# Experts of a mixture layer ranked by token count on the chip, with full jobs of 128 slots and half jobs of 64 slots in turn

## The reference

```python
def _swiglu(h, w_gate, w_up, w_down):
    return (jax.nn.silu(h @ w_gate) * (h @ w_up)) @ w_down

def _moe(h, w_router, b_router, w_gate, w_up, w_down):
    logits = (h @ w_router).astype(jnp.float32) + b_router.astype(jnp.float32)
    top_vals, top_idx = lax.top_k(logits, TOP_K)
    wts = jax.nn.softmax(top_vals, axis=-1)
    combine = jnp.sum(jax.nn.one_hot(top_idx, N_EXPERTS) * wts[..., None], axis=-2)
    out = jnp.zeros_like(h)
    for e in range(N_EXPERTS):
        out = out + combine[..., e:e + 1] * _swiglu(h, w_gate[e], w_up[e], w_down[e])
    return out
```

## Time and profile before

| | value |
|---|---|
| runs | 2107.23, 2112.40, 2112.99 us; median 2112.4 |
| the profiled execution: span from first to last instruction | 2107.7 us |
| TensorE busy (matmul) | 2035.7 us, 97% |
| VectorE busy | 1439.6 us, 68% |
| ScalarE busy | 1148.5 us, 54% |
| GpSimd busy | 130.5 us, 6% |
| moved by DMA | 526.67 MB, mean 250 GB/s |
| granted TensorE clock, mean | 0.992 |
| a job, from one output to the next | 97.9 to 98.0 us |

### The profile page before, as it was taken

One profiled execution on the slowest core, in us unless ns is written; L12 is line 12 of the kernel. 1 busy time (PEld: TensorE's weight loads), 2 busy tenths in 40 slices (PEclk: granted clock), 3 DMA queues, 4 the chain that ended last, 5 costly groups with the idle time before them and its releaser, 6 DMA issues. The chain is left out here.

```text
span 2107.7 us, 34719 instructions
## 1 busy us (share of the span) xinstructions
PE 2035.7 (97%) x13413; PEld 1830.5 (87%) x13413; DVE 1439.6 (68%) x1595; ACT 1148.5 (54%) x1162; POOL 130.5 (6%) x170
## 2 busy tenths in 40 slices
PE   7999999999999999999999899999999999999997
PEld 5999999888999889989999688888888888888885
DVE  4477445555444455755454699898989898988987
ACT  4433334444333443432443568686868677776865
POOL 3100003200000030000230100000000000000000
PEclk9999999999999999999999999999999999999998
DMA  9634465654766454435654599999999999999996
GB/s 352 213 91 155 129 205 174 203 179 131 219 200 215 136 164 147 122 103 171 184 184 164 189 325 398 327 393 328 380 347 367 358 349 376 326 394 319 403 326 252
DMA packets 244081, 526.67 MB, mean 250 GB/s; under 512 B 18151, under 2 KB 142169, under 8 KB 243970
## 3 DMA queue, kind: packets, MB, share of 16 engines
q1 hardware_dynamic: 234304, 495.78, 67.0%
q0 software_dynamic: 9648, 29.29, 4.5%
q10 hardware_dynamic: 18, 0.04, 0.0%
HBM read 512.44 MB, written 12.59 MB: 249 GB/s over the span
## 5 line engine op out<-in xcount | busy, mean ns | idle before, releaser
L1688 ACT ACTIVATE mhi<-mraw 128x2048 fp32r<-128x2048 f32 (+1 forms) x318 | 574.0, 1819 | 210.5 <-DMA mraw<-in_w_exp_up 72.9
L1157 DVE TENSOR_TENSOR mlo<-mraw,mhi 128x2048 fp32r<-128x2048 f32 (+1 forms) x317 | 677.1, 2163 | 15.7 <-ACT mhi L1688 14.8
L571 DVE TENSOR_TENSOR wlo<-raw,whi 128x1024 fp32r<-128x1024 f32 x244 | 289.1, 1212 | 314.8 <-ACT whi L1397 313.6
L1973 PE MATMUL ps<-h1h,whi 128*128 128x320 f32 x1248 | 385.1, 321 | 8.8 <-DVE h1l L678 3.9
L1974 PE MATMUL ps<-h1l,whi 128*128 128x320 f32 x1248 | 370.7, 309 | 0.0
L2469 PE MATMUL ps<-mhi,xeh 128*128 128x512 f32 (+1 forms) x864 | 326.7, 378 | 1.8 <-DVE xel L1176 1.7
L2470 PE MATMUL ps<-mhi,xel 128*128 128x512 f32 (+1 forms) x864 | 321.3, 372 | 0.0
L1397 ACT ACTIVATE whi<-raw 128x1024 fp32r<-128x1024 f32 x244 | 247.8, 1046 | 118.9 <-PE ps L2358 44.9
L1973 PEld LDWEIGHTS ps<-h1h,whi 128*128 128x128 f32 x1248 | 235.3, 189 | 25.3 <-issue 18.7
L1974 PEld LDWEIGHTS ps<-h1l,whi 128*128 128x128 f32 x1248 | 235.5, 189 | 0.0
L2475 PE MATMUL ps<-mlo,xeh 128*128 128x512 f32 (+1 forms) x864 | 224.5, 371 | 0.0
(11 more groups left out here) (415 smaller groups left out, 2657.1 us busy)
## 6 DMA issues: line engine op xcount, KB each, us to landing
mraw<-in_w_exp_down SPq DMA_DIRECT2D x198, 512.0 KB, 8.6
mraw<-in_w_exp_gate SPq DMA_DIRECT2D x150, 512.0 KB, 5.5
mraw<-in_w_exp_up SPq DMA_DIRECT2D x144, 512.0 KB, 6.5
raw<-in_w_in SPq DMA_DIRECT2D x128, 512.0 KB, 3.9
raw<-in_w_ada SPq DMA_DIRECT2D x64, 512.0 KB, 3.8
mraw<-in_w_exp_gate SPq DMA_DIRECT2D x72, 384.0 KB, 3.6
mraw<-in_w_exp_up SPq DMA_DIRECT2D x72, 384.0 KB, 4.6
pause<-in_w_ada SPq DMA_DIRECT2D x32, 512.0 KB, 6.8
```

Of the source, the lines that this page charges most:

```text
L571: V.tensor_tensor(WLO[:, u % RAW_UNITS, 0:w], RAW[:, u % RAW_UNITS, 0:w], WHI[:, h % HI_UNITS, 0:w].bitcast(F32), ALU.subtract).then_inc(l ...
L1157: V.tensor_tensor(MLO[:, n % RAW_RING, 0:w], MRAW[:, n % RAW_RING, 0:w], MHI[:, n % HI_RING, 0:w].bitcast(F32), ALU.subtract).then_inc(m_l ...
L1688: A.activation(MHI[:, n % HI_RING, 0:w], MRAW[:, n % RAW_RING, 0:w], ACT.Copy).then_inc(m_hi, 1)
L1973: M.matmul(out_, w, v[0], start=start, stop=False, skip_group_check=True)
```

## The change

1. The seven experts 1 to 7 are ranked by count on the chip. Job 0 is expert 0 as before, with 128 slots. Jobs 2, 4, 6 take the three fullest with 128 slots; jobs 1, 3, 5, 7 the four others with 64 slots (`half`). An expert with more tokens than its slots gets extra jobs of 64 slots (`EXTRA` = 6). Job 7 is run by the conditional loop, which has 1 + `EXTRA` turns.
2. In a half job the high part of the 64 gathered rows stands in columns 0 to 63 of the stationary operand and the low part in columns 64 to 127. One pass over the weights' high part so gives both; with the pass over the low part there are 2 passes in place of 3. Rows 0 to 63 and 64 to 127 of the result are still to be added: the "turn" product multiplies by `FOLD` (two stacked identities) in place of the identity, which adds them while it transposes. So in a half job gate and up are copied raw from PSUM by ScalarE (`SG`, `SU`), folded by TensorE, and silu, the product with up and the split are done on the folded tiles of 64 columns. `choose` for a half job compares with slot numbers 0 to 63, twice over (`IOTAH`).
3. The table of jobs takes nine parts and not five, and starts at pair 2; SyncE waits for it before job 1 and reads the expert of every job.

The diff, cut to what the prediction speaks of:

```diff
-EXTRA = 4
+HALF = 64
+MAIN = NE - 1
+EXTRA = 6
 JOBS = NE + EXTRA
+TURNS = 6
...
-TABLE_PAIRS = {17: 0, 20: 1, 22: 2, 25: 3, 28: 4}
+TABLE_PAIRS = {2: 0, 4: 1, 6: 2, 8: 3, 17: 4, 19: 5, 21: 6, 23: 7, 25: 8}
...
             sp.wait_ge(sem("routed"), 1)
-            extra = sp.value_load(XI[0:1, 4:5], min_val=0, max_val=EXTRA)
-            with sp.Fori(0, EXTRA) as k:
+            with sp.Fori(0, MAIN // 2) as two:
+                for job in (two * 2 + 1, two * 2 + 2):
+                    e = sp.value_load(XI[0:1, bass.ds(job, 1)], min_val=0, max_val=NE - 1)
+                    load_job(job, e)
...
-            def choose(job):
-
+            def choose(job, half):
+
+                slots = IOTAH[:, :] if half else CF[:, C_IOTA:C_IOTA + P]
                 for t in range(TT):
-                    V.tensor_scalar(PM[:, t, :], CF[:, C_IOTA:C_IOTA + P], POSJ[:, t, bass.ds(job, 1)], None,
-                                    ALU.is_equal)
+                    V.tensor_scalar(PM[:, t, :], slots, POSJ[:, t, bass.ds(job, 1)], None, ALU.is_equal)
...
+                if half:
+                    V.tensor_tensor(XEH[:, s, HALF:P], src[:, :, HALF:P], XEH[:, s, 0:HALF].bitcast(F32),
+                                    ALU.subtract).then_inc(xe_out, 1)
...
+            def half_constants():
+
+
+                V.tensor_tensor(FOLD[:, :], CF[:, C_ID:C_ID + HALF], CF[:, C_ID + HALF:C_ID + P], ALU.add)\
+                    .then_inc(sem("fold_made"), 1)
+                V.tensor_copy(IOTAH[:, 0:HALF], CF[:, C_IOTA:C_IOTA + HALF])
+                V.tensor_copy(IOTAH[:, HALF:P], CF[:, C_IOTA:C_IOTA + HALF])
                 V.memset(PRE[:, :, :], 0.0)
-                V.tensor_scalar(CNT[:, 1, :], CNT[:, 0, :], float(P), None, ALU.is_gt)
-                st(V.tensor_scalar(CNT[:, 2, :], CNT[:, 0, :], float(2 * P), None, ALU.is_gt))
-                V.tensor_tensor(CNT[:, 3, :], CNT[:, 1, :], CNT[:, 2, :], ALU.add)
-                st(V.tensor_tensor(PRE[:, 0, 9:16], CNT[:, 1, 0:7], CNT[:, 2, 0:7], ALU.add))
+                V.memset(XF[:, :], 0.0)
+                st(V.scalar_tensor_tensor(KEY[:, 0, :], CNT[:, 0, :], float(NE), CF[:, C_IOTA8:C_IOTA8 + NE],
+                                          ALU.mult, ALU.subtract))
...
+                n = [P, NE, NE]
+                st(V.tensor_tensor(OH[:, 0], KEY[:, 0:1, :].broadcast_to(n), KEY[:, 0, :].unsqueeze(2).broadcast_to(n),
+                                   ALU.is_gt))
+                st(V.tensor_reduce(KEY[:, 1, :], OH[:, 0], AX.X, ALU.add))
+                st(V.tensor_scalar(KEY[:, 2, :], KEY[:, 1, :], 3.5, None, ALU.is_gt))
+                st(V.tensor_scalar(KEY[:, 3, :], KEY[:, 2, :], 7.0, None, ALU.mult))
+                st(V.scalar_tensor_tensor(KEY[:, 3, :], KEY[:, 1, :], 2.0, KEY[:, 3, :], ALU.mult, ALU.subtract))
...
+            def half_low(job, number, k):
+
+
+                f0, nf = tile_at(k)
+                dve.wait_ge(gt_hi, job * TURNS + (k + 1))
+                V.tensor_tensor(GTH[:, f0:f0 + nf, HALF:P],
+                                SGT[:, k % 2, 0:nf * HALF].rearrange("p (k n) -> p k n", k=nf),
+                                GTH[:, f0:f0 + nf, 0:HALF].bitcast(F32), ALU.subtract).then_inc(half_lo, 1)
...
+                        elif what == "turn" and half:
+                            n = tile_at(k)[1] * HALF
+                            dve.wait_ge(gate_out, job * TURNS + (k + 1))
+                            V.tensor_tensor(SGT[:, k % 2, 0:n], SGT[:, k % 2, 0:n], PS[:, bank, 256:256 + n], ALU.mult)\
                                 .then_inc(m_aux_out, 1)
...
-            with dve.Fori(1, NE) as job:
-                job_dve(job)
+            job_dve(0, False, True, first=True)
+            with dve.Fori(0, MAIN // 2) as two:
+                job_dve(two * 2 + 1, True, False, two)
+                job_dve(two * 2 + 2, False, True)
             dve.wait_ge(sem("routed"), 1)
-            extra = dve.value_load(XI[0:1, 4:5], min_val=0, max_val=EXTRA)
-            with dve.Fori(0, EXTRA) as k:
+            extra = dve.value_load(XI[0:1, 15:16], min_val=1, max_val=1 + EXTRA)
+            with dve.Fori(0, 1 + EXTRA) as k:
                 with dve.If(k < extra):
-                    job_dve(k + NE)
-            dve.wait_ge(m_aux_out, extra * JAUX + (NE * JAUX + AHEAD))
-            dve.wait_ge(xe_out, extra * 2 + (NE * 2 + 2))
+                    job_dve(k + MAIN, True, True, k + MAIN // 2)
...
+            def half_high(job, k, s):
+
+
+                f0, nf = tile_at(k)
+                act.wait_ge(m_aux_out, job * JAUX + (AHEAD + s + 1))
+                A.activation(GTH[:, f0:f0 + nf, 0:HALF],
+                             SGT[:, k % 2, 0:nf * HALF].rearrange("p (k n) -> p k n", k=nf), ACT.Copy).then_inc(gt_hi, 1)
...
+                    if half and p < GPAIRS and p % KD == KD - 1:
+                        g, w = p // KD, GROUPS[p // KD][1]
+                        for i in range(2):
+                            act.wait_ge(m_tile, job * 9 + (3 * g + 1 + 2 * i))
+                            A.activation(SG[:, i, 0:w], PS[:, GROUP_BANKS[g][2 * i], 0:w], ACT.Copy)
+                            if i == 0:
+                                act.wait_ge(m_tile, job * 9 + (3 * g + 2))
+                            else:
+                                act.wait_ge(m_used, job * PAIRS + (p + 1))
+                            A.activation(SU[:, i, 0:w], PS[:, GROUP_BANKS[g][2 * i + 1], 0:w], ACT.Copy)\
+                                .then_inc(prod_made, 1)
...
+                        if what == "turn" and half:
+                            n = tile_at(k)[1] * HALF
+                            act.wait_ge(m_aux_in, job * JAUX + (s + 1))
+                            if k >= 2:
+                                act.wait_ge(half_lo, number * TURNS + (k - 1))
+                            A.activation(SGT[:, k % 2, 0:n], PS[:, 4 + s % 2, 0:n], ACT.Silu).then_inc(gate_out, 1)
...
                             M.matmul(o_, XEH[:, k, :], hi_[:, s], start=(k == 0), stop=False)
-                            M.matmul(o_, XEL[:, k, :], hi_[:, s], start=False, stop=False)
+                            if not half:
+                                M.matmul(o_, XEL[:, k, :], hi_[:, s], start=False, stop=False)
...
                                 M.matmul(PS[:, DOWN_BANKS[h], :], GTH[:, kf, :], hi_[:, s], start=(kf == 0), stop=False)
-                                M.matmul(PS[:, DOWN_BANKS[h], :], GTL[:, kf, :], hi_[:, s], start=False, stop=False)
+                                if not half:
+                                    M.matmul(PS[:, DOWN_BANKS[h], :], GTL[:, kf, :], hi_[:, s], start=False, stop=False)
...
+                            for m in range(tile_at(k)[1] if half else 0):
+                                for j, raw in enumerate((SG, SU)):
+                                    c0 = 256 * j + m * HALF
+                                    ins = M.matmul(PS[:, bank, c0:c0 + HALF], raw[:, k % 2, m * P:(m + 1) * P],
+                                                   FOLD[:, :], start=True, stop=True, skip_group_check=True)
...
```

192 lines of the change are left out of this document (123 added, 69 removed).

## The result

The changed kernel takes 2099.1 us in the median of four runs (2098.3 to 2101.7), the kernel before 2111.8 us beside it: ratio 0.9945, 95% interval 0.993 to 0.9959. It is 12.7 us faster where 36.7 were forecast, and 2099.1 lies inside the range.

A forecast was written before the change was run, and what follows sets the result against it. The prediction took TensorE to set the pace, with VectorE and DMA close behind. Five half jobs saving 48.5 us, less 1.0 for job 0 and 10.8 at the end, gave -36.7 us: 2076 us, range 2044 to 2108.

The forecast's parts named there:

- The half job's time: Step for each 64-slot job: VectorE's 83.9 us plus waits of 1.4 and 3.0 give 88.3 us, bounds 84 and 96.
- TensorE in a half job: Step on TensorE's work in a 64-slot job: it falls from 98.0 to 70.7 us and stops being the bound.
- VectorE in a half job: Step on VectorE's work in a 64-slot job: 87.4 less 8.9 plus 5.4, so 83.9 us, highest by busy time.
- The handoffs: Term in the 64-slot job: 0.5 us of waiting for each of six turned tiles passed between engines, 3.0 us.
- The data rate: Step on weight loads: 410 GB/s from the trace, 85.6 us for 35.1 MB, against the page's 358 GB/s.
- The full jobs: Step on the 128-slot jobs: nothing changes, TensorE still needs 98.0 us, no gain counted.
- The end: Term after the last job: two more leftover gathers, 9.4 us, and two more empty turns, 1.4, together 10.8 us.
- The handoffs' case: Rival for 64-slot jobs: handoffs between three nearly full engines cost twice as much, 94 us a job, 2104 in all; 17%.
- The ring's slack across jobs: Rival: the load ring carries slack between jobs, a full and a half job together take 174 us, 2026 in all; 7%.
- 348 GB/s: Rival: gate and up loads are held to this rate, 95.7 us a half job, 2113 in all, no change; 6%.
- Another count: Rival: an expert of 63 or 62 tokens exceeds 64 on the chip, a tenth job of 88 us, 2159; 2%.
- The clock: Rival: TensorE's clock falls in half jobs as it idles between pairs, 141 us a job at 1.2 GHz, 2340; 6%.

The follow-up runs named there:

- e13: Changed kernel, but in half jobs VectorE makes 32 low-part columns per block and TensorE's second pass rereads the high part: 2101.63 us, half jobs 94.1.
- e5: Changed kernel, but in half jobs each pair's second transfer brings only 128 columns, about half the bytes: 2059.49 us, half jobs 84.7.
- e14: Changed kernel, but in half jobs SyncE waits for one more used pair, a ring of six slots: 2138.42 us, half jobs 101.1.
- e11: Changed kernel, but in half jobs VectorE makes its eight adds two steps earlier: 2102.95 us, half jobs 94.9.
- e17: As e13, with ScalarE's raw copies at group ends cut to 64 columns: 2087.7 us, half jobs 90.2.
- e8: Changed kernel run again unaltered for a second profile: 2101.92 us, half jobs 93.2.
- e3b: Changed kernel with every job run as a full job of 128 slots in 3 passes: 2127.67 us, ratio 1.007 to the kernel before.
- e10: Changed kernel with the loop of three turns over two jobs written out on the four engines: 2096.88 us, ratio 0.9923 to the kernel before.
- e9: Changed kernel, but half jobs make and use the low part for 32 columns per block only, skipping the rest of the low pass: 2108.87 us, half jobs 96.5.
- e7: Changed kernel, but in half jobs TensorE runs 24 extra products into an unused bank after pair 4: 2106.29 us, half jobs 94.6.

## Why the prediction was wrong

**The step that failed is "The half job's time"**: that VectorE, highest by busy time, sets it, and that only its own handoff waits, 4.4 us, come on top. The half job is 93.4 us, 5.1 over the forecast. Five such jobs are 25.5 us, more than the 23 by which the median missed. What holds in its place: the half job is the time that 35.1 MB take through a ring of seven slots whose holder TensorE is. Shown of this are that VectorE's amount of work doesn't set it (24.5 us in place of 84.1, and the job is no shorter: e13), that the bytes count (e5), that one slot less costs 7.7 us (e14), and that the missing 7.5 us lie in the gate and up rows, where the loads run at 266 to 381 GB/s. There TensorE is late for two reasons. It stops at the adds and at the copies, and with the first stop gone the second holds the ring (e11). And between them, in pairs 10 to 19, its own work fills the time (e17). How the 7.5 us divide between the two in the changed kernel is argued, not shown. The 85.6 us of the transfers were in the prediction, but only as a time that 83.9 and its waits would cover; the error was to let the two lie over each other for a whole job. While VectorE and TensorE lag in the gate and up rows, the transfers lose time that the down rows, already at 410 GB/s, can't give back.

An estimate shows how little the ring leaves. While outputs are added, TensorE comes to pair 7 only after an add that stands behind the low part of pair 8. In e13 ScalarE begins to round pair 7 as it lands, and SyncE loads into its slot 7.8 us later; pair 15, loaded after a stop with nothing queued ahead of it, lands 5.1 us after its first issue (1912.11, shown above):

```profile
1895.41 1.92 ACT L1775 ACTIVATE mhi<-mraw 128x2048 fp32r<-128x2048 f32 x1 [0.65 <-DMA mraw<-in_w_exp_up]
...
1903.19 0.33 SPq L536 DMA_DIRECT2D mraw<-in_w_exp_gate  x1
...
1917.24 1.91 ACT L1775 ACTIVATE mhi<-mraw 128x2048 fp32r<-128x2048 f32 x1 [1.52 <-DMA mraw<-in_w_exp_up]
```

With VectorE's full low part, 2.0 us longer, a slot is thus in use for 5.1 + 7.8 + 2.0 = 14.9 us at least. At 410 GB/s seven 1.049 MB slots come round in 7 x 2.56 = 17.9 us, six in 15.4. Seven leave 3.0 us and six 0.5, and a stop of 3.7 us is more than either. That is argued, not shown.

**TensorE in a half job** was undersized. A turn of four tiles is eight products, and takes 1.70 us (in e13 from 1919.40 to 1921.10), so 22 tiles take 9.4 us and not 6.0. The trace has two instructions for each of these full-precision products, 88 for 44. So the row that the forecast divided, 4.4 us in 32, stands for 16 products:

```profile
L2652 PE MATMUL ps<-fold,su 128*128 128x64 f32 x44 | 8.5, 275 | 0.0
L2652 PE MATMUL ps<-fold,sg 128*128 128x64 f32 x44 | 8.4, 272 | 0.0
```

That makes 74 us of work and not 70.7. Sixteen of the 22 tiles are turned beside pairs 10 to 19, 6.8 us of work in the stretch where the loads run slow and TensorE is busy 5.00 of 5 us in five of the six windows. The forecast expected gaps before the low pass; a sum over the whole job hid that in this stretch there are hardly any.

**VectorE in a half job**, 83.9: right, 84.1. The turned tiles of 256 columns take 0.42 us (forecast 0.41). **ScalarE**, 77: 73.4; its busy time is no matter, its order at the copies is. **The handoffs**, 3.0: VectorE waited 2.6 + 1.8 us at turned tiles, and 3.1 us at low parts for rounded pairs, which the sum had not; the first kind is 1.1 us when less data have to come (e5).

**The data rate.** 410 was right as the rate with free slots (409 to 415 in every window from 1936 to 1971 us), and wrong as the mean. By the 358 GB/s that the Trainium skill, DMA: Bandwidth & Descriptors, Specifications, gives a core as its share, a half job would be 98.1 us, an estimate; the trace disagrees with it, with 377 in the mean and 410 where nothing holds it. Only one core runs here, and no run shows two.

**The full jobs**, nothing: 97.0 to 97.8 for 97.9, a gain of 1.9 us in three. It isn't the half jobs' doing: the second profile (e8) has nothing in sum, and with all jobs full (e3b) jobs 2, 6 and 8 take 97.0 to 97.2 too. **Job 0**, 1: 0.8. **The end**, 10.8: 11.0. **The loops** were not in the sum at all. A turn with two jobs' code costs TensorE 2.3 to 2.8 us of issue at its start, and e10 shows the gap gone without the loop. With full jobs the new structure costs 4.6 us in the jobs (e3b); with half jobs e10's 2.2 us aren't clear of nothing.

**The rivals.** The handoffs' case came nearest in number (94 us, 2104) and is wrong in mechanism: it priced a copy block and turned tiles as VectorE's delays, and e5 shows these small. But the copy block that it named is one of the two stops; what it delays is TensorE, and so the ring. The ring's slack across jobs: out, half jobs are longer and not shorter than the forecast. 348 GB/s: out (e9). Another count: out, nine jobs ran. The clock: in the changed kernel 0.66 in one window of job 7 and 0.97 in the mean, which costs nothing that e7 could find; but with less work for TensorE it comes, 0.50 for 24 us in e9. The Trainium skill, TensorE: Matmul & The Clock Gate, Why this matters for your kernels, warns of long pauses between bursts, and the 0.66 after the wait of 3.67 us agrees with it. In e9 no wait before the fall was longer than 2.0 us, so the forecast's reading that short gaps are harmless doesn't hold.

**Open**: how the last 4.6 us of a half job, from the 90.2 of e17 to the transfers' 85.6, divide between TensorE's own work beside pairs 10 to 19, which fills the slow stretch, and the ring's length, which might have bridged it. A ring of eight slots or a run with fewer turned products in that stretch would tell; neither was tried.

## What to carry to other kernels

When an edit brings several engines and the transfers to within 10% of each other, the largest busy time is a floor and not a forecast: ask stage by stage which is behind, how many buffers lie between the first and the last of them, and what frees a buffer. Making the ring one slot shorter is a cheap experiment that tells at once whether it binds (here 7.7 us in 93.4). An engine that frees buffers should wait for nothing that stands, in another engine's list, behind work on a later buffer; where two such waits follow each other, removing one may show no gain. And look at that engine's busy share where the transfers slow down, not only in the mean (here 25.0 of 25 us, in a job where it has 9 to spare).

## What the runs showed of the hardware

- TensorE's granted clock read 0.66 in the 5-us window after a wait of 3.67 us, and 0.50 for 24 us in e9, after 24 us in which it was busy 17.4 and waited at most 2.0 at a time; in e7, with the long wait filled, it read 1.00 throughout job 7.
- The transfers of one core kept up 409 to 415 GB/s for 35 us on end with loads of 512 KB.
- Indirect gathers that run one after the other at the end cost 4.5 to 6.3 us each, from issue to issue (2072.20 to 2092.68 us).
- A full-precision float32 product of 64 columns is two instructions in the trace and took 0.21 us in a row of eight (1.70 us).
- Going round a loop whose body is two jobs long left TensorE 2.3 to 2.8 us without instructions; written out, the gap is gone (e10).
